# Attention stage of a two-layer trunk: small transfers on GpSimd's queue, shared rope, a third score buffer and a longer lag

## The reference, cut to what matters

```python
q = rope((hn @ w_q).reshape(bsz, t, N_HEADS, HEAD_DIM), pos)          # 16 heads of 128
gates = jax.nn.sigmoid(hn @ w_gate + b_gate)                          # 3 branches x 16 heads
o_cmp, p_grp = cmp_branch(q, pos, kv['k_cmp'], kv['v_cmp'])           # compressed rows
idx, ok = select_blocks(p_grp, pos, kv['n_slc'])
o_slc = kv['slc_fn'](q, pos, idx, ok)                                 # selected blocks
o_win = kv['win_fn'](q, pos)                                          # window of 512
o = gates[:, :, 0] * o_cmp + gates[:, :, 1] * o_slc + gates[:, :, 2] * o_win
```

## Time and profile before

| | |
| --- | --- |
| median of 3 runs | 3507.39 us (3506.57 to 3511.26) |
| the profiled execution, its own time | 3512.62 us |
| its span | 3510.5 us |
| mean granted clock of TensorE | 0.969 |
| busy share of the span | PE 94%, PEld 89%, DVE 57%, ACT 42%, POOL 14% |
| chain of waits, by line | L381, L382 and L383 21% each |
| the attention stage | about 2050 to 2483 us of the span |

### The profile page before, as it was taken

One profiled execution on the slowest core, in us unless ns is written; L12 is line 12 of the kernel. 1 busy time (PEld: TensorE's weight loads), 2 busy tenths in 40 slices (PEclk: granted clock), 3 DMA queues, 4 the chain that ended last, 5 costly groups with the idle time before them and its releaser, 6 DMA issues.

```text
span 3510.5 us, 71373 instructions
## 1 busy us (share of the span) xinstructions
PE 3315.6 (94%) x27932; PEld 3140.6 (89%) x27932; DVE 2011.3 (57%) x2301; ACT 1486.1 (42%) x1957; POOL 477.2 (14%) x414
## 2 busy tenths in 40 slices
PE   7999999999899999999989987988899999999998
PEld 6988899899899999999889975744889999999987
DVE  6999888855544444445664544344454444444565
ACT  4555555533444433343444421233344443343342
POOL 5665565500000000000000000000000000000000
PEclk9999999999999999999999998988899999999998
DMA  6444444455465556655455557776646555656543
GB/s 176 137 148 143 149 146 145 137 170 176 140 188 179 180 180 180 180 180 180 147 165 181 166 181 220 252 236 209 203 155 179 175 185 180 180 173 187 180 155 109
DMA packets 379239, 608.11 MB, mean 173 GB/s; under 512 B 52489, under 2 KB 137050, under 8 KB 378746
## 3 DMA queue, kind: packets, MB, share of 16 engines
q1 hardware_dynamic: 349930, 544.10, 50.3%
q10 hardware_dynamic: 28320, 59.81, 5.3%
q0 software_dynamic: 768, 1.22, 0.1%
HBM read 594.83 MB, written 26.94 MB: 177 GB/s over the span
## 4 chain that ended last, share of the span: by engine, by line
PE 72%; DVE 12%; issue 5%; POOL 4%; ACT 3%; DMA 2%; SPq 1%; ACTq 0%; POOLq 0%; DVEq 0%
PE psum L381 21%; PE psum L383 21%; PE psum L382 21%; DVE rows_rest L1257 2%; DVE turned L1316 1%; PE psum L2198 1%; DMA w_raw<-in_cache_slc_k 1%; PE psum L2249 1%; POOL prod_pool L1466 1%; PE psum L2096 1%; PE psum L2208 1%; DVE state_ri L1324 1%; ACT scores_p L2152 1%; PE psum L2084 1%; POOL sines L1415 1%
## 5 line engine op out<-in xcount | busy, mean ns | idle before, releaser
L366 DVE TENSOR_TENSOR w_rest<-w_raw,w_head 128x1024 fp32r<-128x1024 f32 x776 | 977.7, 1272 | 1051.9 <-ACT w_head L362 1051.7
L362 ACT ACTIVATE w_head<-w_raw 128x1024 fp32r<-128x1024 f32 x776 | 812.6, 1057 | 1062.8 <-PE psum L383 1032.5
L381 PE MATMUL psum<-act_head,w_head 128*128 128x264 f32 x4224 | 1210.1, 286 | 30.4 <-DVE act_rest L433 24.8
L383 PE MATMUL psum<-act_head,w_rest 128*128 128x264 f32 x4224 | 1206.5, 286 | 0.0
L382 PE MATMUL psum<-act_rest,w_head 128*128 128x264 f32 x4224 | 1205.0, 285 | 0.0
L381 PEld LDWEIGHTS psum<-act_head,w_head 128*128 128x128 f32 x4224 | 802.0, 190 | 34.9 <-issue 33.0
L382 PEld LDWEIGHTS psum<-act_rest,w_head 128*128 128x128 f32 x4224 | 804.1, 190 | 0.0
L383 PEld LDWEIGHTS psum<-act_head,w_rest 128*128 128x128 f32 x4224 | 802.3, 190 | 0.0
L381 PE MATMUL psum<-hid_head,w_head 128*128 128x264 f32 x1408 | 401.0, 285 | 0.0
L383 PE MATMUL psum<-hid_head,w_rest 128*128 128x264 f32 x1408 | 400.6, 285 | 0.0
L382 PE MATMUL psum<-hid_rest,w_head 128*128 128x264 f32 x1408 | 399.9, 284 | 0.0
(11 more groups left out here) (378 smaller groups left out, 4135.8 us busy)
## 6 DMA issues: line engine op xcount, KB each, us to landing
w_raw<-in_ffn_w_gate SPq DMA_DIRECT2D x176, 512.0 KB, 4.0
w_raw<-in_ffn_w_up SPq DMA_DIRECT2D x176, 512.0 KB, 4.3
w_raw<-in_ffn_w_down SPq DMA_DIRECT2D x176, 512.0 KB, 3.9
w_raw<-in_cache_cmp_k SPq DMA_DIRECT2D x256, 128.0 KB, 2.6
w_raw<-in_cache_cmp_v SPq DMA_DIRECT2D x256, 128.0 KB, 2.6
w_raw<-in_ssm_w_glu SPq DMA_DIRECT2D x64, 512.0 KB, 3.8
w_raw<-in_ple_w_gate SPq DMA_DIRECT2D x64, 512.0 KB, 4.3
w_raw<-in_kv_w SPq DMA_DIRECT2D x48, 512.0 KB, 3.9
```

The lines of the kernel that those rows point to most:

```text
L362: nc.scalar.activation(WH[:, u.slot, :], RAW[:, u.slot, :], ACT.Copy).then_inc(head_done, 1)
L366: nc.vector.tensor_tensor(WL[:, u.slot, :], RAW[:, u.slot, :], WH[:, u.slot, :].bitcast(F32), ALU.subtract).then_inc(rest_done, 1)
L381: nc.tensor.matmul(o, WH[:, u.slot, w], heads[:, k, :], start=k == 0, stop=False)
L383: last = nc.tensor.matmul(o, WL[:, u.slot, w], heads[:, k, :], start=False, stop=k == UK * kunits - 1)
```

## The change

On PE `own_rows_pe` is called inside `gates_pe`, ahead of its eleventh slice. `own_rows_dve` clears `QZ` first. A new program `attention_pool` on GpSimd issues the masks, the gate rows, the other constants and the `W2P` pieces, does two of the three rope operations, and issues the own rows and the row outputs; SyncE keeps the tiles and the two taps, now at u = 6 and u = 20 and without a wait. A third score buffer lets the turn of an item lag by two items and its outputs by three. `QZ`, `RK` and `PART` lie elsewhere in SBUF.

```diff
+    SP2X = sb("scores_p2", [P, HREP, TP], at=scratch)
...
-    RK = sb("rank_pairs", [P, 2, 30, 30], at=wl_at + PAST * 4)
+    RK = sb("rank_pairs", [P, 2, 30, 30], at=hn_at + 4 * TP * 4)
+    QZ = sb("q_spread", [P, TS * QSTEP], at=wl_at + PAST * 4)
...
-    PART = sb("rope_part", [P, 4 * TP], at=wh_at)
+    PART = sb("rope_part", [P, 4 * TP], at=hn_at)
...
         for k in range(KC):
+            if k == 10:
+                own_rows_pe(pe)
...
         dve.wait_ge(free_b, by_name["o"].groups)
+        V.memset(QZ[:, :], 0.0).then_inc(new_done, 1)
...
-        dve.wait_ge(gates_done, 1)
-        V.memset(QZ[:, :], 0.0).then_inc(new_done, 1)
...
+    def rope_pool(pool, j):
+        dst = ROPED[j]
+        cos = ROPET[:, 0, 0:TP].unsqueeze(1).to_broadcast([P, 4, TP])
+        pool.wait_ge(sw_done, j + 1)
+        nc.gpsimd.tensor_tensor(dst, dst, cos, ALU.mult).then_inc(rope_cos, 1)
+        pool.wait_ge(sw_used, j + 1)
+        pool.wait_ge(rope_cos, j + 1)
+        nc.gpsimd.tensor_tensor(dst, dst, PART[:, :].rearrange("p (h t) -> p h t", h=4), ALU.add).then_inc(rope_done, 1)
...
+        if j == 0:
+            dve.wait_ge(rope_done, len(ROPED))
...
+    def prompt_rows(k):
+        return SP2[:, k % 3, :, :] if k % 3 < 2 else SP2X[:, :, :]
...
-        if k >= 2:
-            dve.wait_ge(pt_done, k - 1)
+        if k >= 3:
+            dve.wait_ge(pt_done, k - 2)
...
-        if stage == 1 and 1 <= k <= len(ITEMS):
-            prompt_turn_pe(pe, k - 1)
-        if stage == 2 and 2 <= k <= len(ITEMS) + 1:
-            prompt_outputs_pe(pe, k - 2)
+        if stage == 1 and 2 <= k <= len(ITEMS) + 1:
+            prompt_turn_pe(pe, k - 2)
+        if stage == 2 and 3 <= k <= len(ITEMS) + 2:
+            prompt_outputs_pe(pe, k - 3)
...
-            if 1 <= k <= len(ITEMS):
-                prompt_take_act(act, k - 1)
+            if 2 <= k <= len(ITEMS) + 1:
+                prompt_take_act(act, k - 2)
...
-        if stage == 0 and k >= 5 and (k - 5) % 3 == 0 and (k - 5) // 3 < len(ITEMS) // 3:
-            prompt_out_dve(dve, (k - 5) // 3)
+        if stage == 0 and k >= 6 and k % 3 == 0:
+            prompt_out_dve(dve, k // 3 - 2)
...
+    def attention_pool(pool):
+        pool.wait_ge(gates_done, 1)
+        for dst, name in ((BD, "bd"), (TOB, "toblk"), (SAME, "same"), (EARL, "earlier")):
+            pool.dma_start(dst[:], io["k_" + name]).then_inc(ld_masks, 16)
+        gate_rows_pool(pool)
+        for dst, name in ((CAUS, "causal"), (CMPV, "cmpvis"), (ROPP, "ropep")):
+            pool.dma_start(dst[:], io["k_" + name]).then_inc(ld_vis, 16)
+        pool.dma_start(W2P[:, 0, :], io["cmp_k_w2"]).then_inc(ld_second, 16)
+        pool.dma_start(W2P[:, 1, 0:64], io["cmp_k_w2"][:, 64:128]).then_inc(ld_second, 16)
+        pool.dma_start(W2P[:, 1, 64:128], io["cmp_k_w2"][:, 0:64]).then_inc(ld_second, 16)
+        pool.dma_start(W2P[:, 2, :], io["cmp_v_w2"]).then_inc(ld_second, 16)
+        for j in range(len(ROPED)):
+            rope_pool(pool, j)
+        own_rows_pool(pool)
+        for j in range(len(ROW_JOBS)):
+            rows_pool(pool, j)
+        pool.wait_ge(rows_stored, ROWS_STORED)
+        pool.wait_ge(nat_stored, NAT_STORED)
+
...
     def attention_sp(sp):
         for t in range(RING):
             load_tile(sp, t)
         sp.wait_ge(gates_done, 1)
-        for dst, name in ((BD, "bd"), (TOB, "toblk"), (SAME, "same"), (EARL, "earlier")):
-            sp.dma_start(dst[:], io["k_" + name]).then_inc(ld_masks, 16)
         for t in range(RING, TILES):
             if not by_act(t):
                 load_tile(sp, t)
             u = t - WK - RING
-            if u == 3:
-                gate_rows_sp(sp)
-            if u == 9:
-                own_rows_sp(sp)
-            if u == 12:
-                for dst, name in ((CAUS, "causal"), (CMPV, "cmpvis"), (ROPP, "ropep")):
-                    sp.dma_start(dst[:], io["k_" + name]).then_inc(ld_masks, 16)
-            if u == 26:
-                sp.wait_ge(rope_done, len(ROPED))
+            if u == 6:
                 sp.dma_start(W1P[:, :, :], w1[0].rearrange("t d h -> d t h")).then_inc(ld_taps, 16)
-                sp.dma_start(W2P[:, 0, :], io["cmp_k_w2"]).then_inc(ld_taps, 16)
-                sp.dma_start(W2P[:, 1, 0:64], io["cmp_k_w2"][:, 64:128]).then_inc(ld_taps, 16)
-                sp.dma_start(W2P[:, 1, 64:128], io["cmp_k_w2"][:, 0:64]).then_inc(ld_taps, 16)
-                sp.dma_start(W2P[:, 2, :], io["cmp_v_w2"]).then_inc(ld_taps, 16)
-            if u == 34:
+            if u == 20:
                 sp.dma_start(W1Q[:, :, :], w1[1].rearrange("t d h -> d t h")).then_inc(ld_taps, 16)
-            if 33 <= u < 57 and u % 2:
-                rows_sp(sp, (u - 33) // 2)
```

More of the change, by code:

```diff
@@ L1798, in trunk_kernel @@
     att_used = sem("att_used")
-    ld_gate, ld_masks, ld_taps, ld_kc, ld_vc, gates_moved = (
-        sem(n) for n in ("ld_gate", "ld_masks", "ld_taps", "ld_kc", "ld_vc", "gates_moved"))
+    ld_gate, ld_masks, ld_vis, ld_taps, ld_second, gates_moved = (
+        sem(n) for n in ("ld_gate", "ld_masks", "ld_vis", "ld_taps", "ld_second", "gates_moved"))
     rows_stored = sem("rows_stored")
@@ L1813, in before_kv_sp @@
         sp.dma_start(BGATE[0:48, 0:1], io["nsa_b_gate"][0].rearrange("(p a) -> p a", a=1)).then_inc(ld_gate, 16)
-    L_MASKS_FIRST, L_MASKS, L_TAPS = 16 * 4, 16 * 7, 16 * 6
+    L_MASKS, L_VIS, L_TAPS, L_SECOND = 16 * 4, 16 * 3, 16 * 2, 16 * 4
     def tile_slot(t):
@@ L1916, in rope_dve @@
     def rope_dve(dve, j):
-        dst = ROPED[j]
-        cos, sin = (ROPET[:, k, 0:TP].unsqueeze(1).to_broadcast([P, 4, TP]) for k in range(2))
+        sin = ROPET[:, 1, 0:TP].unsqueeze(1).to_broadcast([P, 4, TP])
         dve.wait_ge(sw_done, j + 1)
@@ L1921, in rope_dve @@
             dve.wait_ge(rope_done, j)
[L1922 to L1927, removed]
+        V.tensor_tensor(PART[:, :].rearrange("p (h t) -> p h t", h=4), PSUM[:, SIDE[0]:SIDE[1] + 1, :].rearrange("p b (h t) -> p (b h) t", h=2),
+                        sin, ALU.mult).then_inc(sw_used, 1)
+    def rope_pool(pool, j):
[6 more added lines that the diff above has]
+        nc.gpsimd.tensor_tensor(dst, dst, PART[:, :].rearrange("p (h t) -> p h t", h=4), ALU.add).then_inc(rope_done, 1)
     def small_rows_pe(pe, j):
@@ L2005, in prompt_taps_pe @@
             pe.wait_ge(ld_taps, L_TAPS)
+            pe.wait_ge(ld_second, L_SECOND)
         rows = KVT[:, kv, :, 0:TP].rearrange("p g (n s) -> p s g n", s=STRIDE)
@@ L2035, in prompt_keys_dve @@
         pc_pe.wait(dve, "k second")
-        dve.wait_ge(ld_masks, L_MASKS)
+        dve.wait_ge(ld_vis, L_VIS)
         V.tensor_tensor(RTP[:, 0:NPC], PSUM[:, SIDE[0], 128:128 + NPC], ROPP[:, 1, :], ALU.mult)
@@ L2083, in prompt_turn_pe @@
             for r in range(HREP):
-                last = nc.tensor.transpose(PSUM[0:w, PROBS_BANK + kc, r * P:(r + 1) * P], SP2[:, k % 2, r, kc * P:kc * P + w], IDENT[:, :])
+                last = nc.tensor.transpose(PSUM[0:w, PROBS_BANK + kc, r * P:(r + 1) * P], prompt_rows(k)[:, r, kc * P:kc * P + w], IDENT[:, :])
         last.then_inc(pt_done, 1)
@@ L2102, in prompt_mask_dve @@
         n = keys_of(item)
-        s = SP2[:, k % 2, :, 0:n]
+        s = prompt_rows(k)[:, :, 0:n]
         mask = CMPV[:, qt, :] if br == 0 else CAUS[:, qt, 0:n]
@@ L2149, in prompt_exp_act @@
         for r in range(HREP):
-            s = SP2[:, k % 2, r, 0:n]
+            s = prompt_rows(k)[:, r, 0:n]
             at = 16 * (k % 2)
@@ L2535, in attention_dve @@
         own_rows_dve(dve)
-        dve.wait_ge(ld_masks, L_MASKS_FIRST)
+        dve.wait_ge(ld_masks, L_MASKS)
         V.memset(ZERO[:, :].bitcast(F32), 0.0)
@@ L2743, in _ @@
         gates_pool(pool)
+        attention_pool(pool)
         ffn_pool(pool, 1)
```

22 lines of the change are left out of this document (10 added, 12 removed).

## The result

The changed kernel took 3480.51 us (median of 4 runs, 3474.15 to 3481.66) beside 3509.32 us of the kernel before: ratio 0.9913, interval 0.9896 to 0.993. In a second comparison, with other runs of both, it was 3480.41 beside 3516.27 us, ratio 0.9904 (0.988 to 0.9928). The gain is 29 to 36 us; 60 were forecast. By the two profiled executions it is 38.5 us (3512.62 to 3474.15): in both comparisons the profiled execution of the changed kernel was 6 us shorter than its other runs (3474.29 beside 3479.77 to 3483.45).

The account below looks back on a forecast made before the run. PE bounds the kernel, transfers close behind. Stretch gains summed to 66.8 us, less 7 kept back for PE's clock: 60, from 3512.6 to 3452.6, less 5.2 for the profiled run: 3447 us; range 3424 to 3484.

Parts of the forecast that it names:

- A: Attention key steps 0 to 11: 31 us against 33.8, gain 2.8, with gate rows on GpSimd and first taps load moved in.
- V2: Second half of the prompt items beside the value tiles: 18.2 us a group, 73 against 89.9 us, gain 17.
- What is late next, three candidates: Value steps: PE's own work, tiles (15.0 us a group), or the serial VectorE-ScalarE loop of mask, maximum, exponentials, probabilities (17.1).
- V1: First half of the prompt items beside the value tiles: held by tiles, 67 against 79.6 us, gain 12.5.
- 60, plus 7 for its beginning: V1: 60 us held by tiles, plus 7 for first-probabilities wait moved to third item's scores and sample's own scores.
- Start: Start of the attention stage: spread-query wait goes, last mask lands at 2065.5 rather than 2063.0; gain 2.0 us.
- masks landing after 2068: Start of attention, last mask's landing time in us: listed as a sign that the prediction is wrong.
- B: Key steps 12 to 23 with six rope jobs: sharing rope with GpSimd gives 33 us, gain 10.5.
- C: Key steps 24 to 54 with row outputs: 66 us against 82.3 without taps and row outputs on SyncE, gain 16.3.
- Rival 1: All attention stretches: transfers bound at today's 276 GB/s; gain only 38 us, 3469 us; chance 0.18.
- Rival 2: Value steps: lag meets the next wait, in-order ScalarE-VectorE coupling; they give 12 not 35, total gain 37, 3470 us; chance 0.12.
- Rival 3: Step 8: GpSimd's gate rows stop VectorE and PE; at 6 us a piece 4 us slower, 3511 us; chance 0.03.

Follow-up runs that it names:

- e5_quarter_first: Changed kernel with finished outputs copied ahead of the next probabilities and only 32 of 128 partitions of each value tile loaded: 3453.90 us, ratio 0.9835.
- e8_three: Changed kernel with masks on SyncE, finished outputs copied ahead of the next probabilities, and taps loads cut in pieces at steps 12 to 23: 3442.84 us, ratio 0.9815.

## Why the prediction was wrong

- *The sum.* It had 67 before the reserve and 60 after it, against 37 by stretches and 29 to 36 by medians. Most of what lies between the last two is the changed kernel's profiled execution, 6 us shorter than its others. What was listed as gone did go; what came late next had no term, or too small a one, in A, the value steps and the start.
- *A, forecast +2.8, measured -6.5.* The failed step is "28.2 us at 314 GB/s": it spread the taps' bytes evenly over twelve steps. They come as a burst that costs 12 us, and the lower bound, both stalls of the taps as in the earlier trace rows, left out the half clock behind it (3.6 us). By the cuts here the forecast is 26.9 us with the taps in it, and A takes 24.4 to 24.8 without them. The gate rows' part held: 6.9 us.
- *V2, forecast 17, measured 9.7.* The failed step is "What is late next, three candidates": PE, tiles and the loop were weighed, the single output bank was not. Its copy lay in VectorE's order behind a probability that is now no longer late for PE. With the copy first V2 gains 20.8 us and takes the 17.5 us a group that PE's own work was worked out to need (17.4).
- *V1, forecast 12.5, measured -0.2.* The output bank has only 2.1 of PE's 16.3 us of idle time here; tiles have 10.5. The failed step is the term "60, plus 7 for its beginning": V1 takes 71 to 79 us in the runs of this order, and 71.3 with a quarter of the tiles' bytes and the copy first, so the bytes are not what holds it. The wait did move to the third item's scores, as forecast, but the beginning was under-sized by the clock behind its stop. How much of V1's rest that is stays open.
- *Start, forecast 2.0, measured -0.8.* The wait for the spread queries went as worked out. The failed step is the landing of the last mask, "at 2065.5 rather than 2063.0": it priced GpSimd's issues, 0.54 us each, nearly as they came (0.55 to 0.61), but not the window tiles that the earlier own rows let SyncE issue ahead of the mask. Counted from the last gate matmul the mask landed at 10.4 us, where 7.4 was taken and 4.9 had been. In the time of the kernel before that is 2068.5, so the sign "masks landing after 2068" came.
- *B and C, right.* Rope's pairs were 4.7 us and the price 2.36 each. The Trainium skill, "SBUF — State Buffer", "Who interferes with whom", says that a VectorE instruction with two SBUF inputs contends with GpSimd's reads, and one with at most one, outside the 2-port modes, does not. This case's trace agrees: 2.27 us in place of 0.16 for the small product of two SBUF columns, no GpSimd operation over 2.38 us, and key copies as short as ever. In C only the size was right (63.3 to 70.2 us against 66): I gave the row outputs' queue a part of it, and put back on SyncE they cost nothing. The Trainium skill, "DMA: Bandwidth & Descriptors", "Issuing engines are not separate DMA queues", says that starting transfers from several engines saves only the time of the start, and the row outputs agree: C takes 64.5 us with them on SyncE.
- *The rivals.* Rival 1 has a near number (38, against 37 by the sum) by luck: its ceiling of 276 GB/s is refuted by 326 GB/s in A and 332 in B with the taps in pieces. Rival 2 (37) said that the lag meets the next wait, and it does: V1 to tail gain 16.4 us, where it had 12. But the wait is for the output bank, and the coupling that it named does not show with the copy first. Rival 3's wait exists, 2.2 us of VectorE at step 8 and 1.9 us of PE behind it, where the forecast had nothing, and is far from deciding.

## What to carry to other kernels

When a wait on an engine is removed, go through every buffer that this engine writes next, and see where in the other engine's program the release of each one stands; a release behind work that waits for a third engine is the next wait. A large load on a queue that also feeds a stream is a burst, not an average: cut it to pieces no larger than the stream's own and place it where the stream has room. An edit that lets one engine run earlier also brings its transfers ahead of others: look which landing falls behind them. Price a new wait with the slower clock behind it, not by its own length.

## What had not been expected of the hardware

- Twelve microseconds at a DMA share of 1.01 to 1.05 carried 326 GB/s; pieces among tiles carried 332 over 31 us. Window tiles and the mask carried 416 at the start of the kernel after, so the 314 GB/s of the prediction is no ceiling:

```profile
2063.00:2067.00 4.00, 2.67 (x12) 1.91 (x10) 0.08 (x1) 0.00 (x0) 0.00 (x0) 0.50 1.02 416
```

- The same mask of 450 KB landed 3.3 to 3.7 us after its issue ahead of the window tiles, by SyncE or by GpSimd, and 7.8 to 9.1 us after one behind three of them.
- A VectorE operation on one column took 2.27 us in place of 0.16 beside a GpSimd operation, when both read two operands from SBUF.
- After a stop of 3.4 us the clock stayed at its lower level for 22 us in one execution (`e5_quarter_first`), with PE busy all but 1.4 of them. After one of 4.7 us in `e8_three` it was 0.51 from 2255.6 to 2260.2 us and 1.00 from there to 2264.
- The profiled execution of the changed kernel was 6 us faster than the others, twice; why stays open.
